# A decoder layer on one Trainium2 core: the up projection of the gated MLP as seven block products in place of eight, its gated output kept in DRAM

## The reference, cut to what matters

```python
def conv_ffn(h, conv_prev, w_ffn_in, conv_w, conv_b, w_down):
    T = h.shape[1]
    a, up = jnp.split(h @ w_ffn_in, [D_FF], axis=-1)
    ext = jnp.concatenate([conv_prev.astype(a.dtype), a], axis=1)
    conv = conv_b + sum(conv_w[j] * ext[:, j:j + T] for j in range(CONV_W))
    return (jax.nn.silu(conv) * up) @ w_down, ext[:, T:]
```

## Time and profile before

| | us |
|---|---|
| median of 3 runs | 1656.25 |
| lowest and highest | 1654.29, 1657.55 |
| span of the profiled execution | 1651.3 |
| TensorE (matmul) busy in it | 1573.0 |
| VectorE busy | 740.3 |
| ScalarE busy | 554.4 |
| GpSimd busy | 162.0 |

### The profile page before, as it was taken

The page is one execution under the profiler, slowest core; times in us unless marked ns, Lnnn a source line. Parts: engine busy times, 40 slices in busy tenths (PEclk is TensorE's granted clock), DMA queues, the critical chain, the costliest instruction groups (busy, mean ns, idle before and its releaser), DMA issues.

```text
span 1651.3 us, 26400 instructions
## 1 busy us (share of the span) xinstructions
PE 1573.0 (95%) x10653; PEld 1332.1 (81%) x10653; DVE 740.3 (45%) x1333; ACT 554.4 (34%) x1093; POOL 162.0 (10%) x265
## 2 busy tenths in 40 slices
PE   6999998899999999989999999999999999999994
PEld 6989996556666655558889999999999998876683
DVE  7524204654555555556653322232232324354495
ACT  2246123632565533351113222222222224332341
POOL 2100001200000135311110000000000000000020
PEclk9999998898999999999999999999999999999997
DMA  7312012010000267651231111111111116334381
GB/s 250 105 35 82 26 52 81 5 51 22 19 12 17 103 220 260 204 186 65 89 104 52 38 51 47 41 46 43 51 38 51 38 64 204 122 122 146 106 259 71
DMA packets 90481, 147.66 MB, mean 89 GB/s; under 512 B 5546, under 2 KB 62504, under 8 KB 90360
## 3 DMA queue, kind: packets, MB, share of 16 engines
q1 hardware_dynamic: 75562, 93.94, 18.1%
q0 software_dynamic: 14688, 52.43, 9.3%
q10 hardware_dynamic: 144, 0.07, 0.0%
HBM read 130.70 MB, written 15.72 MB: 89 GB/s over the span
## 4 chain that ended last, share of the span: by engine, by line
PE 68%; DVE 2%; ACT 2%; issue 1%; DMA 1%; POOL 0%; SPq 0%; ACTq 0%; POOLq 0%; DVEq 0%
PE ps L210 17%; PE ps L212 17%; PE ps L211 17%; PE ps L1268 4%; PE ps L1619 3%; PE ps L1598 2%; PE ps L1305 2%; PE ps L1645 2%; PE ps L1282 2%; PE ps L2482 1%; DMA ring_c<-in_cache_ckv,row_at 1%; ACT sprob L1706 1%; DVE sst_m L1781 1%; PE ps L2012 0%; PE ps L1631 0%
## 5 line engine op out<-in xcount | busy, mean ns | idle before, releaser
L210 PE MATMUL ps<-h1T_hi,f_hi 128*128 128x352 f32 (+1 forms) x1056 | 342.4, 324 | 0.7 <-DVE h1T_lo L1941 0.7
L212 PE MATMUL ps<-h1T_hi,f_lo 128*128 128x352 f32 (+1 forms) x1056 | 341.3, 323 | 0.0
L211 PE MATMUL ps<-h1T_lo,f_hi 128*128 128x352 f32 (+1 forms) x1056 | 340.6, 323 | 0.0
L210 PEld LDWEIGHTS ps<-h1T_hi,f_hi 128*128 128x128 f32 x1056 | 198.2, 188 | 1.0 <-DVE h1T_lo L1941 0.9
L211 PEld LDWEIGHTS ps<-h1T_lo,f_hi 128*128 128x128 f32 x1056 | 198.2, 188 | 0.0
L212 PEld LDWEIGHTS ps<-h1T_hi,f_lo 128*128 128x128 f32 x1056 | 198.1, 188 | 0.0
L210 PE MATMUL ps<-w_hi,hT_hi 128*128 128x256 f32 (+2 forms) x504 | 141.8, 281 | 3.3 <-DVE hT_lo L324 3.3
L210 PE MATMUL ps<-d_hi,g_hi 128*128 128x512 f32 x352 | 141.3, 401 | 1.2 <-issue 1.2
L212 PE MATMUL ps<-w_hi,hT_lo 128*128 128x256 f32 (+2 forms) x504 | 141.2, 280 | 0.0
L2207 DVE TENSOR_TENSOR f_lo<-f_raw,f_hi 128x1024 fp32r<-128x1024 f32 x44 | 53.7, 1221 | 194.9 <-ACT f_hi L2161 194.9
L211 PE MATMUL ps<-w_lo,hT_hi 128*128 128x256 f32 (+2 forms) x504 | 141.1, 280 | 0.0
(11 more groups left out here) (309 smaller groups left out, 2645.8 us busy)
## 6 DMA issues: line engine op xcount, KB each, us to landing
d_raw<-in_w_down SPq DMA_DIRECT2D x66, 512.0 KB, 3.6
f_raw<-in_w_ffn_in SPq DMA_DIRECT2D x88, 256.0 KB, 3.2
w_raw<-in_w_in SPq DMA_DIRECT2D x6, 1024.0 KB, 5.3
xs<-in_x_prompt SPq DMA_DIRECT2D x8, 512.0 KB, 3.9
h_res<-xs POOLq DMA_DIRECT2D x8, 512.0 KB, 3.3
wo_raw<-in_w_o SPq DMA_DIRECT2D x2, 2048.0 KB, 8.8
hr<-h_res SPq DMA_DIRECT2D x8, 512.0 KB, 3.6
h_res<-hr POOLq DMA_DIRECT2D x8, 512.0 KB, 3.0
```

The lines of the kernel that those rows point to most:

```text
L210: nc.tensor.matmul(out, ah, bh, start=start, stop=False)
L211: nc.tensor.matmul(out, ah, bl, start=False, stop=False)
L212: return nc.tensor.matmul(out, al, bh, start=False, stop=stop)
```

## The change

The product of the weights of a chunk (a 2 x 2 arrangement of blocks: inner half h by result u) with `h1T` (inner half by half of the 1060 tokens, 530 each) is formed by Winograd's variant of Strassen's scheme. With A the weight blocks (`a11`, `a21` of result a and up in inner half 0; `a12`, `a22` in half 1) and B the token blocks, it takes seven products of block sums in place of eight products of blocks. Each product has 2 blocks of tokens (266 and 264 columns), 4 blocks of k and 3 matmuls: 24 matmuls, 168 in a chunk. They run in the order q = 0 to 6 and accumulate in three pairs of PSUM banks (`ACC`: 0/1, 2/3, 4/5, 2/3, 0/1, 4/5, 2/3). Partial results are taken out of a pair between two products that add to it, with the sums still in it. Chunk 0 is computed as before, with blocks of 354, 354 and 352.

The sums of token blocks (`t_sum`, 4 of 128 x 2120 elements) are made once, on VectorE and GpSimd, from `h1T_hi` + `h1T_lo` (`raw_block`), and split again. The sums of weight blocks (`s_sum`, 4 of 128 x 512 a chunk) are made on GpSimd. ScalarE and VectorE split seven operands of 128 x 512 a chunk, in place of two of 128 x 1024. ScalarE copies product 0 to `p1`; VectorE forms `u2`, `u3` and the outputs with five pairs of additions that read PSUM. The taps and the gating of chunk c-1 run during chunk c. The gated output goes to a buffer in SBUF (`gst`, 128 x 1056) and from there to a DRAM tensor, `g_res`; `gT` is gone. In stage h each of the 66 steps also loads its tokens of `g_res`, and the decode columns are loaded once.

```diff
+        FIRST_UP = N_META - 4
+        UP = ((FIRST_UP, 354), (FIRST_UP + 354, 354), (FIRST_UP + 708, 352))
+        HALF = (T - FIRST_UP) // 2
+        SUB = ((0, 266), (266, 264))
...
+            raw_block(dve, nc.vector, 0, 1)
             h1_lo(NT - 1)
...
+        a11, a21 = f_raw[0][:, :, 0, :], f_raw[0][:, :, 1, :]
+        a12, a22 = f_raw[1][:, :, 0, :], f_raw[1][:, :, 1, :]
+        s_sum = [at(f"s_sum{i}", [P, 4, P], E0 + 113312 + 2048 * i)[:, :, :] for i in range(4)]
+        op_hi = [at(f"op_hi{q}", [P, 4, P], E0 + 8192 + 4096 * q, F32R) for q in range(7)]
+        op_lo = [at(f"op_lo{q}", [P, 4, P], E0 + 10240 + 4096 * q, F32R) for q in range(7)]
+        t_hi = [at(f"t_hi{j}", [P, 4, HALF], E0 + 36864 + 8480 * j, F32R) for j in range(4)]
+        t_lo = [at(f"t_lo{j}", [P, 4, HALF], E0 + 70784 + 8480 * j, F32R) for j in range(4)]
+        t_sum = [at(f"t_sum{j}", [P, 4, HALF], E0 + 70784 + 8480 * j) for j in range(4)]
...
-        gT = at("gT", [P, FC, T], E0 + 33600)
...
+        u2, u3, p1 = gap_hi[:, 0, GAP], gap_hi[:, 1, GAP], gap_hi[:, 2, GAP]
+        gst = gap_lo[:, 0:2, FIRST_UP + HALF:FIRST_UP + HALF + (NS + SEQ) // 2]
+        up = gap_lo[:, 2:4, GAP]
+        g_res = nc.dram_tensor("g_res", (FC, P, NS + SEQ), F32, kind="Internal").ap()
...
+        B_OF = ((0, 0), 1, 0, 2, (1, 0), (1, 1), 3)
+        T_READY = (None, 2, 2, 4, None, None, 4)
+        ACC = (0, 2, 4, 2, 0, 4, 2)
+        FIRST_IN = (True, True, True, False, False, False, False)
+        OP_OF = (a11, s_sum[1], s_sum[0], s_sum[2], a12, s_sum[3], a22)
+        S_OF = (0, 2, 2, 3, 0, 4, 0)
...
+        def store_gated(sp, c):
+            sp.wait_ge(g_done, c + 1)
+            sp.dma_start(g_res[bass.ds(c, 1), :, :].rearrange("a p (b t) -> p (a b) t", b=2), gst).then_inc(g_stored, 16)
...
-            with sp.Fori(0, FC - 1) as c:
-                for h in range(2):
-
-                    sp.wait_ge(f_split, 2 * c + (h + 1))
-                    load_unit(sp, c + 1, h)
+            for h in range(2):
+                sp.wait_ge(op_split, h + 1)
+                load_unit(sp, 1, h)
+            with sp.Fori(1, FC - 1) as c:
+                sp.wait_ge(s_done, 4 * c)
+                sp.wait_ge(op_split, split_count(c, 0))
+                load_unit(sp, c + 1, 0)
+                sp.wait_ge(op_split, split_count(c, 6))
+                load_unit(sp, c + 1, 1)
+                store_gated(sp, c - 1)
             sp.wait_ge(h1_turned, 2 * NT)
             for m in range(2):
                 load_d(sp, m)
+            store_gated(sp, FC - 2)
...
-            def chunk(c):
-                for h in range(2):
-                    pe.wait_ge(f_split, 2 * c + (h + 1))
-                    for u in range(2):
-                        if h == 0:
-
-                            after_chunks(pe, (ext_ready, g_done)[u], c)
-                        for b, (c0, n) in enumerate(UP):
-                            for k in range(4):
-                                last = mm3(ps[:, 3 * u + b, 0:n], [x[h][:, k, u, :] for x in (f_hi, f_lo)],
-                                           [x[:, 4 * h + k, c0:c0 + n] for x in (h1T_hi, h1T_lo)],
-                                           h == 0 and k == 0, h == 1 and k == 3)
-                        if h == 1 and u == 0:
-                            last.then_inc(a_mm, 1)
-                    last.then_inc(f_used, 1)
+            def product(c, q):
+                pe.wait_ge(op_split, split_count(c, q))
+                if T_READY[q]:
+                    pe.wait_ge(t_split, T_READY[q])
+                if q == 0:
+                    pe.wait_ge(x_out, ext_count(c - 1))
+                elif q == 1:
+                    pe.wait_ge(acc_out, acc_count(c - 1, C21))
+                elif q == 3:
+                    pe.wait_ge(acc_out, acc_count(c, U2))
+                elif q == 4:
+                    pe.wait_ge(x_out, p1_count(c))
+                elif q == 5:
+                    pe.wait_ge(acc_out, acc_count(c, C22))
+                for s, (c0, n) in enumerate(SUB):
+                    for k in range(4):
+                        (ah, al), (bh, bl) = (op_hi[q][:, k, :], op_lo[q][:, k, :]), b_part(q, h1T_hi, h1T_lo, k, c0, n)
+                        o = ps[:, ACC[q] + s, 0:n]
+                        again = not FIRST_IN[q]
+                        nc.tensor.matmul(o, ah, bh, start=FIRST_IN[q] and k == 0, stop=False, skip_group_check=again)
+                        nc.tensor.matmul(o, ah, bl, start=False, stop=False, skip_group_check=again)
+                        last = nc.tensor.matmul(o, al, bh, start=False, stop=k == 3, skip_group_check=again)
+                last.then_inc(prod_done, 1)
...
+        def silu(act, c):
+            act.wait_ge(conv_dve, 2 * c + 2)
+            nc.scalar.activation(conv[:, :], conv[:, :], ACT.Silu).then_inc(conv_act, 1)
...
             def body(c, more):
+                act.wait_ge(prod_done, product_count(c - 1, 6))
+                op_high_part(act, c, 6)
+                act.wait_ge(prod_done, product_count(c, 0))
+                act.wait_ge(acc_out, acc_count(c - 1, C21))
+                for s, (c0, n) in enumerate(SUB):
+                    last = nc.scalar.activation(p1[:, c0:c0 + n], ps[:, s, 0:n], ACT.Copy)
+                last.then_inc(x_out, 1)
                 if more:
+                    op_high_part(act, c + 1, 0)
+                silu(act, c - 1)
+                if more:
+                    for q in range(1, 4):
+                        act.wait_ge(prod_done, product_count(c, q))
+                        op_high_part(act, c + 1, q)
                 else:
+                    act.wait_ge(op_split, split_count(c, 6))
                     step_high(act, 0)
+                act.wait_ge(prod_done, product_count(c, 4))
+                act.wait_ge(new_kept, c)
                 nc.scalar.activation(ext[:, 0:EXT].rearrange("p (b j) -> p b j", b=DEC_B)[:, :, 2:],
                                      ps[:, 0, 0:NS].rearrange("p (b t) -> p b t", b=DEC_B), ACT.Copy)
+                nc.scalar.activation(ext[:, EXT:EXT + 232], ps[:, 0, 34:266], ACT.Copy)
+                nc.scalar.activation(ext[:, EXT + 232:EXT + 496], ps[:, 1, 0:264], ACT.Copy).then_inc(x_out, 1)
                 if more:
+                    op_high_part(act, c + 1, 4)
+                    act.wait_ge(prod_done, product_count(c, 5))
+                    op_high_part(act, c + 1, 5)
+                else:
+                    step_high(act, 1)
+                act.wait_ge(g_done, c)
+                tap(act, c)
...
+        def raw_block(eng, ops, j, n):
+            eng.wait_ge(h1_split, 2 * (NT - n))
+            ops.tensor_tensor(b_raw[j, n][:, :, :], quarter(h1T_hi, j, n).bitcast(F32), quarter(h1T_lo, j, n).bitcast(F32),
+                              add).then_inc(t_pool if j else t_dve, 1)
+        def late_tap(dve, c, j):
+            if j:
+                dve.wait_ge(conv_act, 2 * c + 1)
+            else:
+                dve.wait_ge(conv_dve, 2 * c + 1)
+            nc.vector.scalar_tensor_tensor(out=conv[:, :], in0=ext[:, j:j + LC],
+                                           scalar=vcol[:, bass.ds(c + V_ROWS["conv_w"] + j * FC, 1)],
+                                           in1=conv[:, :], op0=mult, op1=add).then_inc(conv_dve, 1)
+        def gated_up(dve, c):
+            dve.wait_ge(conv_act, 2 * c + 2)
+            dve.wait_ge(acc_out, acc_count(c, C21))
+            if not (isinstance(c, int) and c == 0):
+                dve.wait_ge(g_stored, 16 * c)
+            n = (NS + SEQ) // 2
+            nc.vector.tensor_tensor(gst[:, 0, 0:NS].rearrange("p (b t) -> p b t", b=DEC_B),
+                                    conv[:, 0:EXT].rearrange("p (b j) -> p b j", b=DEC_B)[:, :, 0:DEC_T],
+                                    up[:, 0, 0:NS].rearrange("p (b t) -> p b t", b=DEC_B), mult)
+            m = HALF - NS - N_META_UP
+            nc.vector.tensor_tensor(gst[:, 0, NS:NS + m], conv[:, EXT:EXT + m], up[:, 0, NS + N_META_UP:HALF], mult)
+            nc.vector.tensor_tensor(gst[:, 0, NS + m:n], conv[:, EXT + m:EXT + n - NS], up[:, 1, 0:n - NS - m], mult)
+            nc.vector.tensor_tensor(gst[:, 1, :], conv[:, EXT + n - NS:LC], up[:, 1, n - NS - m:HALF], mult).then_inc(g_done, 1)
 
...
+            raw_block(dve, nc.vector, 0, 0)
+            dve.wait_ge(old_turned, 1)
+            dve.wait_ge(t_dve, 2)
+            nc.vector.tensor_tensor(t_sum[0][:, :, :], b_raw[0, 1][:, :, :], b_raw[0, 0][:, :, :], sub).then_inc(t_dve, 1)
+            dve.wait_ge(t_dve, 3)
+            dve.wait_ge(t_pool, 1)
+            nc.vector.tensor_tensor(t_sum[1][:, :, :], b_raw[1, 1][:, :, :], t_sum[0][:, :, :], sub).then_inc(t_dve, 1)
+            dve.wait_ge(t_dve, 4)
+            t_low_part(0, 1)
+            op_low_part(dve, 1, 0)
+            op_low_part(dve, 1, 1)
+            dve.wait_ge(t_pool, 3)
+            t_low_part(1, 2)
+            dve.wait_ge(prod_done, 1)
```

(77 more changed lines are left out.)

245 lines of the change are left out of this document (148 added, 97 removed).

## The result

The kernel after takes 1624.93 us (median of four runs, 1622.75 to 1625.89); the kernel before, run beside it, 1655.27 (1652.37 to 1657.55). The ratio is 0.9819, with a 95% interval of 0.9804 to 0.9833: 1.8% faster, 30.3 us. The forecast was 1615, with a range of 1598 to 1640. Sign and range hold, and the gain is 11 us smaller than the 41 us of the sum.

A forecast was written before the change was run, and what follows sets the result against it. TensorE's matmul stream was taken to bound the up projection. The span 1651.3 - 60.7 (fewer matmuls) + 19.6 (ramp) gave 1610.2 us; with 4.95 for the runs' median, 1615 us, range 1598 to 1640.

The forecast's parts named there:

- the 41 us of the sum: Whole kernel: 60.7 us saved in the up projection, less 19.6 us lost in the ramp.
- What bounds the stage: Up projection: lasts as long as TensorE's stream of matmuls, busy 514.34 of 515.30 us; three other engines have room.
- The price of a matmul: New products' matmuls: 0.1210 us each (0.1204 to 0.1215), a chunk of 20.33 us, 21 chunks saving 60.7 us.
- The turns: Ramp: VectorE and GpSimd wide instructions strictly alternate, each waiting for the other's to end; 19.6 us lost, steady chunks 0.
- side by side: Rival in the ramp: VectorE and GpSimd run simultaneously, only 5.5 us lost, 1601 us in all; chance 0.25.
- GpSimd's price: GpSimd additions: two MEMSETs' price, 1.05 us (0.53 to 1.6) for 512 columns, 3.8 (1.9 to 5.7) for 2120.
- The ramp: Token-block sums and splits ahead of chunk 1: product 3 of chunk 1 late by 19.6 us (10.5 to 28.9).
- a wait before product 3 of chunk 1 and little elsewhere: Sign for the ramp: where TensorE's waiting would appear in the trace.
- The steady chunk's slack: Steady chunks: product 3 has 1.2 us left, product 5 0.95, other waits 1.8 or more; TensorE never waits, 0 us.
- The down projection and the seam: Stage h's added loads and stores, and steps 0 and 1 split during the last chunk: cost 0 each.

The follow-up runs named there:

- experiment 3: Kernel after with each product's two token blocks cut 256 and 274 columns instead of 266 and 264: 1650.10 us, ratio 0.9814 to the kernel before.
- experiment 4: Kernel after with most taps, SiLU, gating and GpSimd weight-sum work left out of the up projection: 1647.48 us in one run.
- (6): Kernel before with its up projection token blocks starting at columns 16, 368 and 720 instead of 14, 368 and 720: 1656.60 us in one run.
- experiments 1 and 2: 1: kernel after, GpSimd's four wide ramp instructions moved to VectorE, ratio 0.9782. 2: kernel after, each replaced by two GpSimd MEMSETs, 1640.49 us.
- experiment 8: Kernel after with each of GpSimd's weight sums in the loop made twice: 1644.03 us in one run.
- experiment 5: Kernel after with one SiLU of one element on ScalarE ahead of the loop: 1623.19 us, ratio 0.9806 to the kernel before.
- experiments 5 and 7: 5: as under experiment 5. 7: kernel after with chunk 1 also as eight products and all wide sums on VectorE, 1604.04 us, ratio 0.9698.

## Why the prediction was right, and where its sizes were off

- **What bounds the stage**: right. TensorE's stream sets 20.685 us a chunk, with no wait from 912 to 1337 us.
- **The price of a matmul**: the first term that was mis-sized. It put 0.1210 us (0.1204 to 0.1215) and was 0.1231, outside its bounds; 21 x 168 x 0.0021 = 7.4 us. Two steps made this. The smaller one is the reading of 0.1169 for 0.1173 us (experiment 3), about 1.4 us of the 7.4. The larger one took proportion "between these two sizes" from 256 columns in the input projection and 352 in the up projection. The up projection's own prices at 256 to 354 columns fit 8.7 ns and 0.433 ns a column, and the input projection's 256 columns lie 2.3 ns below; taking both as points of one line hid the fixed part. Not width (experiment 3), not the work that experiment 4 left out, not the start of a block off the 32-byte phase (6) is the cause of those 2.3 ns; what it is stays open. An untested difference is in the operands: the 256 columns that move in the input projection are weights (`w_hi`, `w_lo`), those of the up projection are tokens. The input projection's matmuls of 358 columns, where tokens move, do lie on the line (0.1633 us apart from 120.94 to 121.92, 0.1637 by the fit). The rows did hold a wider bound: the line through 230 and 352 columns gives 111.8 + 35 x 49.1 / 122 = 125.9 ns at 265, where the prediction closed its bounds at 121.5.
- **The turns**: the rule was right, and it was the choice that a row couldn't make. The Trainium skill (SBUF — State Buffer, section Who interferes with whom) says that a VectorE instruction with two SBUF inputs contends with a GpSimd instruction that reads SBUF, not with one that only writes it, and (section SBUF: two separate sides) that whichever starts first gets the shared ports for the whole instruction. The traces agree on each point: 2.37 us beside a MEMSET, 3.35 beside a sum, 6.75 beside a wide one. A pair of additions that take an operand from PSUM keeps its 0.77 us beside a sum (0.78). The rival "side by side", with a chance of 0.25, is excluded by experiments 1 and 2 and by the durations in the ramp.
- **GpSimd's price**: 1.28 us for 512 columns and about 4.4 for 2120, where the prediction took two MEMSETs' price, 1.05 and 3.8; within the bounds, 2.3 to 2.4 MEMSETs. The Trainium skill (GPSIMD Engine Reference, section 3.1 Elementwise) gives 4497 ns for 2048 columns; scaled to these widths, 1.12 and 4.66 us as an estimate, it is above the measured price for the wide and below it for the narrow sum.
- **The ramp**: 22.8 us for 19.6. The place was right, product 3 of chunk 1, 20.3 us late for 19.6. Counted from the end of the last norm, 4.55 us later here than in the prediction's working (860.35 for 855.8), operand 0 is ready at 888.1 for the 886.55 that the turns gave, operand 1 at 893.2 for 891.05, and product 3 starts at 909.36 for 908.45: the order of the turns held step by step. The dearer sums had made it 2.2 us late by operand 1, and VectorE's instructions after that took 1.3 us less than foreseen; that the two partly cancel is luck. The sign given for it, "a wait before product 3 of chunk 1 and little elsewhere", was wrong, and against the prediction's own working, which has operand 0 ready 6.4 us after chunk 0's end: TensorE waits 7.81 us before product 0 and 4.11 before product 1, and 3.88 before product 3. What the sum did not have is the clock: after the last of these waits product 3 runs at the lower level, 5.4 us for 2.96, and costs 2.5 us. A wait of TensorE's had this as a second price.
- **The steady chunk's slack**: right that no product waits. Gating does stretch by one sum (the two-column row), but product 5, where 0.95 us of room was foreseen, does not wait even with four more sums in a chunk: these cost only 0.97 us, and at another wait (experiment 8). The 40 table loads, 2.57 us a chunk on ScalarE, were foreseen by no step and are hidden (experiment 5).
- **The down projection and the seam**: 0 foreseen, 286.8 against 288.0 us measured. The new loads bring DMA from 148 to 190 GB/s, the 42 foreseen. ScalarE waits for `g_raw` three times, 12.3 us in all, where it waited once for `d_raw`, 3.6 us, and this is absorbed.
- **The sum with the sizes as measured**: 1655.27 - 53.2 + 22.8 = 1624.9, and the runs have 1624.93. The interval of the ratio is 4.8 us wide, so the agreement to a tenth says no more than that no large term is missing.

## What to carry to other kernels

Before an algebraic saving is counted in full, price its entry: sums that are made once at a stage's start stand between two stages, and here they took 22.8 of 53.2 us; giving up one of the saving's repetitions (2.5 us) to lay them beside other work, and making them on VectorE alone, brought all of it back. Work given to GpSimd because that engine has room wasn't parallel to VectorE here while VectorE read two operands from SBUF and GpSimd read any: such work had room in the steady chunks, and on the critical ramp VectorE alone was 7.5 us faster. And a matmul's price from another stage carries an error even at the same width (2.3 ns at 256 columns, 6 at 512): where the stage has rows at one width only, bound the price by lines through rows of several stages, since 2 ns a matmul were 7.4 us here.

## What the runs showed of the hardware

- Where VectorE's two-input instructions and GpSimd's reads of SBUF wait for each other, the wait stands inside the durations of both engines and in no view of waits. Its sign is one form with several durations: 2.35, 3.35, 6.17 and 6.75 us for one addition of 2120 columns, or 1.25 us for two columns. On GpSimd a copy of two columns shows 2.33 us for 0.18.
- GpSimd writes 2120 columns in 1.86 us without slowing a two-input VectorE instruction beside it at all (2.37 us).
- TensorE's granted clock is 1.00 before its wait of 7.81 us and 0.50 after it, still 0.50 after the next wait of 4.11, 1.00 some 3 us later, and 0.50 again after the wait of 3.88. The 24 matmuls after the last of them take 5.4 us instead of 2.96, and from 914.74 us on the clock is 1.00.
- With the up projection's first SiLU inside the loop, ScalarE loads a table twice in each of 20 turns, 1283 ns each; with one SiLU ahead of the loop (experiments 5 and 7, and the kernel before) this stage has one load in all.
- 256 columns cost 0.1173 us in the input projection and 0.1197 in the up projection, 512 columns 0.2274 in the output projection and 0.2333 in the down projection, all at a granted clock of 1.00. The cause is not found.
